# Delta rule with queries and key rows side by side as weights, token-major outputs and a tile-wise output norm; residual first in the cross output product

## What is computed

```python
    def step(S, xs):                       # one chunk of 64 tokens, 4 heads
        qc, kc, uc, wc, gcc, ac = xs
        v_new = uc - jnp.einsum('bhck,bhkv->bhcv', wc, S)
        o = (jnp.einsum('bhck,bhkv->bhcv', qc * jnp.exp(gcc)[..., None], S)
             + jnp.einsum('bhij,bhjv->bhiv', ac, v_new))
        g_last = gcc[..., -1]
        S = (S * jnp.exp(g_last)[..., None, None]
             + jnp.einsum('bhck,bhcv->bhkv', kc * jnp.exp(g_last[..., None] - gcc)[..., None], v_new))
        return S, o
...
    oa = rmsnorm(oa, onorm_g) * jax.nn.silu(z_a.astype(f32).reshape(B, L, H_A, DV_A))
    out = jnp.concatenate([oa, ob], axis=-1) @ w_out
...
            xp = xp + cross_attend(rmsnorm(xp, g_cross[layer]), mk, mv, w_xq[layer], w_xo[layer])
            xp = xp + sq_relu_mlp(rmsnorm(xp, g_mlp[layer]), w_up[layer], w_down[layer])
```

## Time and profile before

| | |
|---|---|
| median of 3 runs | 1649.7 us (1646.36 to 1653.46) |
| the profiled execution | 1649.3 us; its span 1647.6 us |
| PE busy | 1595.3 us, 97% |
| DVE, ACT, POOL busy | 663.7, 561.7, 616.4 us |
| mean granted PE clock | 0.987 of full |

### The profile page before, as it was taken

One profiled execution on the slowest core, in us unless ns is written; L12 is line 12 of the kernel. 1 busy time (PEld: TensorE's weight loads), 2 busy tenths in 40 slices (PEclk: granted clock), 3 DMA queues, 4 the chain that ended last, 5 costly groups with the idle time before them and its releaser, 6 DMA issues.

```text
span 1647.6 us, 31601 instructions
## 1 busy us (share of the span) xinstructions
PE 1595.3 (97%) x13455; PEld 1535.2 (93%) x13455; DVE 663.7 (40%) x1233; ACT 561.7 (34%) x949; POOL 616.4 (37%) x513
## 2 busy tenths in 40 slices
PE   6999998999999999999999999999999999999998
PEld 6999987898998999999999998689989999999998
DVE  4484056444435532322223535744254323232234
ACT  5122254324335431312223323643354213131222
POOL 3753201202461444443444532025513534444351
PEclk9999999999999999999999999999999999999999
DMA  5223111003241132322223233012402232322221
GB/s 160 79 77 104 54 54 59 3 2 116 77 156 48 53 103 80 101 78 95 85 79 101 78 103 118 1 37 93 154 26 77 78 103 77 99 81 84 96 77 55
DMA packets 123061, 131.85 MB, mean 80 GB/s; under 512 B 6285, under 2 KB 115122, under 8 KB 122930
## 3 DMA queue, kind: packets, MB, share of 16 engines
q1 hardware_dynamic: 117072, 124.72, 23.4%
q10 hardware_dynamic: 5858, 5.19, 1.0%
HBM read 122.44 MB, written 7.45 MB: 79 GB/s over the span
## 4 chain that ended last, share of the span: by engine, by line
PE 44%; issue 33%; POOL 17%; DVE 3%; ACT 1%; DMA 1%; ACTq 0%; POOLq 0%; DVEq 0%
PE LP L779 36%; POOL wl L673 17%; PE LP L1142 3%; PE MP L923 1%; PE LP L876 1%; DVE xl L2058 1%; DMA stage<-in_w_in_ab 0%; DVE acc L2051 0%; PE MP L897 0%; PE MP L914 0%; DMA stage<-in_w_xq 0%; PE MP L986 0%; PE MP L1142 0%; PE MP L1126 0%; PE MP L1003 0%
## 5 line engine op out<-in xcount | busy, mean ns | idle before, releaser
L673 POOL TENSOR_TENSOR wl<-stage,wh 128x512 fp32r<-128x512 f32 x428 | 576.3, 1378 | 844.8 <-ACT wh L1513 844.7
L779 PE MATMUL LP<-xh,wh 128*128 128x272 f32 x2176 | 458.4, 292 | 11.2 <-DVE xl L2058 7.3
L779 PE MATMUL LP<-xl,wh 128*128 128x272 f32 x2176 | 451.2, 289 | 0.0
L779 PE MATMUL LP<-xh,wl 128*128 128x272 f32 x2176 | 451.1, 289 | 0.0
L779 PEld LDWEIGHTS LP<-xh,wh 128*128 128x128 f32 x2176 | 344.2, 190 | 16.9 <-DVE xl L2058 10.6
L1513 ACT CAST wh<-stage 128x2048 fp32r<-128x2048 f32 x107 | 203.7, 1905 | 441.6 <-PE LP L779 420.5
L779 PEld LDWEIGHTS LP<-xl,wh 128*128 128x128 f32 x2176 | 344.4, 190 | 0.0
L779 PEld LDWEIGHTS LP<-xh,wl 128*128 128x128 f32 x2176 | 342.2, 190 | 0.0
L779 PE MATMUL LP<-hl,wh 128*128 128x272 f32 x1024 | 211.1, 287 | 0.0
L779 PE MATMUL LP<-hh,wh 128*128 128x272 f32 x1024 | 210.6, 287 | 0.0
L779 PE MATMUL LP<-hh,wl 128*128 128x272 f32 x1024 | 210.5, 287 | 0.0
(11 more groups left out here) (391 smaller groups left out, 1634.6 us busy)
## 6 DMA issues: line engine op xcount, KB each, us to landing
stage<-in_w_up SPq DMA_DIRECT2D x32, 1024.0 KB, 5.3
stage<-in_w_down SPq DMA_DIRECT2D x32, 1024.0 KB, 5.1
stage<-in_w_in_ab SPq DMA_DIRECT2D x13, 1024.0 KB, 5.4
...
```

The source lines that it names most:

```text
L673: pool.tensor_tensor(wl[s][:, part], stage[s][:, part], wh[s][:, part].bitcast(f32), ALU.subtract).then_inc(w_lo, 1)
L779: mm = pe.matmul(LP[:, 2 * slot + half, 0:b - a], weights, X[part][:, k, a:b], start=(first and n_ == 0), stop=(last and n_ == 2), skip_gr ...
```

## The change

Four things. First, `wT` becomes `wq`: for each chunk the 64 columns of w and the 64 columns of the scaled queries stand side by side, and one group of 4 matmuls with the state as the moving side gives both, by token: w S in the rows of the chunk, q S in the other 64 rows of the bank. `qs` goes; `o` has `AT` as weights and `vnew` (128 columns) moving and adds to those rows; two banks alternate. ACT copies each chunk out (64 rows) instead of once per tile. Second, the norm is per tile of tokens: ACT squares with a sum over the row (4 heads), Ln and Exp of a 128 x 4 tile, DVE scales the rows, PE turns them (`turn o`), DVE gates, ACT and DVE make the high and low part in `y_split`. All of this but the last tile's is dealt out between the chunks. The blocks k = 0 to 3 read `y_split`, the first 272 tokens apart from the rest. Third, `wq` lies in the weight slots `wh0`, `wh1` and `wl1`, so ACT's cast of panel 1 waits for tile 1 and POOL's low part of panel 1 for the whole recurrence; the two state outputs are issued by SP instead of ACT. Fourth, in `xo` DVE adds the residual before it makes low parts and sums squares, and ACT makes `xh` before it squares.

```diff
+            for j, n_ in zip(OUTS, OUTS[1:]):
+                last = ("ws", n_ + 1, 0) if n_ + 1 < TT else ("o", n_, 1)
+                for where, items in (((("ws", n_, 0)), [norm("sq", j, 0), norm("sq", j, 1)]),
+                                     (("ds", n_, 0), [norm("sq", j, 2), norm("sq", j, 3)]),
+                                     (("o", n_, 0), [norm("rs", j)]), (("ws", n_, 1), [norm("mul", j)]),
+                                     (("ds", n_, 1), [("turn", "o", j), norm("hi", j)]), (last, [norm("lo", j)])):
+                    behind.setdefault(where, []).extend(items)
...
-            recs = [("rec", name, j, c) for j, c in CHUNKS for name in ("ws", "qs", "ds", "o")]
+            recs = recurrence_order()
...
+            low_parts(0, LIN["out0"][0] + 1)
+            pool.wait_ge(rec_pe, 3 * len(CHUNKS))
+            low_parts(1, LIN["out0"][0] + 2)
...
+                    elif kind == "o":
+                        if h == 0:
+                            pe.wait_ge(norm_mul, OUTS.index(j) + 1)
+                        mm = pe.transpose(MP[:, 0, P * h:P * h + P], o_rows[j][0:P, h, :], ident[0:P, 0:P])
...
+                        pe.wait_ge(rec_act, max(q - 1, 1))
...
+                    rows, at = (128, 128 * c) if j < TT else (2 * NS, 0)
                     for h in range(H):
-                        mm = pe.matmul(MP[0:P, 1, 128 * h:128 * h + 128], wT[j][:, h, 0:P], S[:, old, h, :],
-                                       start=True, stop=True, skip_group_check=True)
-                elif name == "qs":
...
-                        mm = pe.matmul(MP[:, 2, P * h + p.start:P * h + p.stop], S[:, old, h, :],
-                                       ua[:, h, a + p.start:a + p.stop], start=(c == 0 and h == 0), stop=False,
-                                       skip_group_check=True)
+                        mm = pe.matmul(state_bank(c)[0:rows, 128 * h:128 * h + 128], wq[j][:, h, at:at + rows],
+                                       S[:, old, h, :], start=(h == 0), stop=False, skip_group_check=True)
...
-                        mm = pe.matmul(MP[:, 2, P * h + p.start:P * h + p.stop], vnew[p, h, :], AT[j][p, h, :],
-                                       start=False, stop=True, skip_group_check=True)
+                        mm = pe.matmul(state_bank(c)[old_rows(j, c), 128 * h:128 * h + 128], AT[j][p, h, :],
+                                       vnew[p, h, :], start=False, stop=True, skip_group_check=True)
...
+            def head_parts(slot, half):
+
+                pe.wait_ge(low_done, NTOK - 1 + half)
...
+                if what == ("rec", "ws", 2, 1):
+                    act.wait_ge(rec_pe, 3 * CHUNKS.index((1, 1)) + 1)
+                    split(1, 16 * (LIN["out0"][0] // 2 + 1))
...
                 for T in range(KT):
+                    residual_tile(f"xo{l}", T)
+                    if T > KT - 4:
+                        low_part(3 * l + 2, T - 5, T - 1)
+                    if T == KT - 1:
+                        low_part(3 * l + 2, 3, KT - 1)
                     if T:
                         accumulate(3 * l + 2, T - 1)
-                    if T > KT - 4:
-                        low_part(3 * l + 2, T - 5, T - 1)
-                    residual_tile(f"xo{l}", T)
-                low_part(3 * l + 2, 3, KT - 1)
                 accumulate(3 * l + 2, KT - 1)
```

260 lines of the change are left out of this document (144 added, 116 removed).

## The result

| | before | after |
|---|---|---|
| median | 1647.99 us (1645.61 to 1653.46, 8 runs) | 1638.24 us (1630.21 to 1640.80, 8 runs) |
| ratio | | 0.9926, 95% interval 0.9903 to 0.9949 |
| profiled execution | 1649.3 us, span 1647.6 us | 1636.7 us, span 1634.9 us |
| mean granted PE clock in it | 0.987 | 0.991 |

The kernel became 9.8 us faster by the medians (0.6%), 12.2 us by the ratio (8.4 to 16.0 by its interval), and 12.7 us by the spans of the two profiled executions. Three lines of the page of the changed kernel: span, PE's busy time, and the granted clock in 40 slices.

A forecast was written before the change was run, and what follows sets the result against it. PE, busy 1595.3 of 1647.6 us, was taken to bound the kernel, so only its work, waits or low-clock time could be won. Gains 1.2 + 0.5 + 5.2 + 3.4 = 10.3 us took 1649.3 to 1639.0 us; range 1631 to 1645.5.

The forecast's parts named there:

- Second inverse: Delta stage: 4.7 us of `qs` go, 1.1 us of output turns and 2.4 us of waits come; gain 1.2 us.
- The price of `o`: Second inverse: between half of `qs`, 0.5 us, and 1.05 us; taken as 0.9 us, even with before.
- The new waits: Second inverse: sample tile's `ds` 1.1 us, turn of values 1.1, ACT's copy 0.4, last inverse steps 0.1; 2.4 us new.
- rival (a): Waits eat the recurrence: turns hold PE, copies late, `o` dear, one more low stretch; 6.5 us back, 1645.5 us; chance 0.20.
- Chunks: Tiles 2 and 3: four chunks sum to 19.25 us; gain 0.5 us if one low stretch stays, 2.2 if none.
- rival (b): Clock stays up: two or more low stretches in inverse, chunks and both `xo` vanish, 1.7 us each; about 1634; chance 0.20.
- Last `o` to panel 1: Tail: tile 3's chain of copy, squares, norm and delta blocks takes 11.2 us against 16.87; gain 5.2 us after DVE-POOL interference.
- the 2.5 us set beside the sum: Tail: by the skill's rule tile 3's scaling and low part could each wait a whole POOL piece, 2.5 us; 1641 us.
- Cross output product: End of `xo`: earlier last residual readies k = 7 sooner, k = 0 comes late next; gain 1.7 us per layer, 3.4 in all.
- Moved past queues: Memory loads and panel 2's cast: cast some 4 us later against PE, covered by 12 us of panel 1.
- Rival (c): Cross output product: residual first does nothing, as squares bind k = 0; 3.4 us less gain, 1642.4 us; chance 0.09.
- (d): Slower: clock stays at 1.2 GHz over 30 us behind tile 2's first `ws`; 22 us more, 1661 us; chance 0.04.

The follow-up runs named there:

- `pool_late`: Changed kernel with POOL's low parts of panel 1 made only behind the last low part of the normed output; 1637.66 us (1 run).
- `delta_alone`: Changed kernel with the old order in the cross output product on DVE and ACT; 1641.48 us, ratio 0.9950 to the kernel before.
- `xo_alone`: Kernel before with only the new order in the cross output product on DVE and ACT; 1641.13 us, ratio 0.9962 to the kernel before.
- the repeat: The changed kernel run and profiled again, unaltered; 1636.48 us, ratio 0.9928 to the kernel before.
- `front_fixed`: Changed kernel with DVE making the sample tile's `vnew` ahead of a query scaling and that tile's output turned one place later; 1631.54 us, ratio 0.9899 to before.
- `all_six`: Changed kernel with six wait-removing edits in DVE's, PE's, POOL's and ACT's order, in delta stage and cross output product; 1629.64 us, ratio 0.9871 to before.

## Why the prediction was right, and where it was not

The forecast was 1639.0 us and 10.3 us of gain; the medians say 1638.24 and 9.8. The terms were less exact than their sum, and that the medians come within 0.8 us is in part luck: the ratio says 12.2 us, and the profiled executions, from which the sum was made, 12.6. At equal clock the stages won 3.65 - 0.5 + 5.83 + 3.46 = 12.4 us where the forecast had 1.2 + 0.45 + 5.2 + 3.4. The signs that it named came: 46.21, 20.20 and 11.04 us, a last turn that waits 1.03, and the wait at k = 0.

- **Second inverse, 1.2 us forecast, 1.96 measured.** Two terms were off and the clock came between. The price of `o` was the worst: 0.9 us, near the upper end. PE's rows in this stage:

```profile
351.43 0.51 PE L1193 MATMUL LP<-Tm,BT 64*64 64x64 f32 x10
351.73 0.32 PE L1289 MATMUL MP<-vnew,AT 64*64 64x128 f32 x1
...
352.74 0.63 PE L1193 MATMUL LP<-TmT,Xm 64*64 64x64 f32 x16
```

Between two inverse steps that take 0.51 us each, eight records of `o` are interleaved, and all three groups take 352.74 - 351.43 = 1.31 us: 0.29 us for `o`. In the first chunk of tile 0, where such a step stands on one side only, it is 0.75 us (337.99 - 336.73, less 0.51). Alone, in the chunks, it takes 389.14 - 388.12 = 1.02 us. Before, it took 1.01 to 1.03 us in this stage, so even 0.9 would have been a small gain. The bound from below, half of `qs`, was not low enough, since it left out that a 64 x 64 group can share PE with another. By the Trainium skill, page TensorE: Matmul & The Clock Gate, section "Part 3: Packing small matmuls — row/col tiling", matmuls in different tiles of the array run at the same time; the trace agrees, with 0.29 us against 1.02. The new waits came where they were said to, at 1.04 (1.1 forecast), 1.12 (1.1) and 0.94 (0.4), with two small ones (0.25, 0.17): 3.5 us against 2.4. At full clock the stage won 45.84 - 42.19 = 3.65 us (an estimate, 3.3 if a stretch is taken at 1.3 us), three times the forecast; a second low stretch, rival (a)'s part, took 1.7 of it. That `o` is cheap because it shares PE is read from these rows; no run tests it by moving `o` alone.
- **Chunks, 0.5 forecast with a low stretch kept, 1.21 measured.** At full clock they went from 19.7 to 20.20 us, a loss of 0.5 where 0.45 of gain was forecast, and the low stretch went, rival (b)'s part. First chunk 4.31 us (4.30 forecast), second 6.58 (6.05: the waits for `vnew`, 0.77, and for POOL's piece, 0.94, add up), third 4.79 (4.55), fourth 4.52 (4.35). What was left out is that `qs` had covered `vnew`, and that `o` alone is 1.02 us against 0.93 before.
- **Last `o` to panel 1, 5.2 forecast, 5.83 measured.** The chain was as written. Copy 1.55 instead of 1.95, squares 1.3 instead of 2.0, DVE beside POOL 0.76 instead of 0.5. `pool_late` found 0.77, so the 2.5 us set beside the sum did not come.
- **Cross output product, 1.7 forecast for each layer, 2.98 and 3.15 measured.** The term itself is exact: 1.73 by `delta_alone` in layer 0. It is so by two small misses that cancel: the way from the last residual to k = 0 took 4.6 us (547.35 to 551.93 in `xo_alone`), not 4.2, and the residual came 0.35 us sooner than forecast; the wait of 0.36 us ahead of the last tile had gone, which the sum left out. I had assumed that the clock falls there as before; with waits of 0.3 to 1.15 us instead of 1.8 it stayed up at both places in all twelve profiles with the new order on DVE. With the old order it fell at three places of four.
- **Moved past queues.** The memory loads went out 3.0 us behind the last `o` (3.7 before), panel 2's cast 2.7 us behind the start of panel 1 (0.6 before), and PE has no wait of 0.3 us or more in panels 1 and 2. The forecast of no cost is not quite safe, though: in the repeat PE waits 0.52 us for memory rows behind panel 1, and by `pool_late` panel 2's cast is ahead of them.
- **The clock.** I named 0.002 of mean clock as what would upset the sum; it moved by 0.004. The profiled change reaches the second inverse 2.2 us later, where nothing was changed: 0.5 us in the first 27 us, and 1.7 by the clock behind them (10.2 us lost against 8.5). The clock cost 1.7 more inside the inverse, and gave 1.7 in the chunks and 1.25 and some 1.4 in `xo`: near nothing in sum. That is luck too.

Rival (c) is out by `xo_alone`. Of (b), three of its four low stretches vanished, and one came in their place. (d) did not occur: with more idle times from tile 2 to panel 1 the clock was at 1.00 there. It fell in these chunks in `front_fixed` and `all_six`, which have no more of them.
